# A transformer layer with routed experts on one core: two raw weight loads ordered behind accumulating transfers

## What is computed

```python
q = (h @ peer_wq).reshape(B, T, PEER_HEADS, PEER_QDIM)        # 8 heads x 256
q1, q2 = q[..., :PEER_HALF], q[..., PEER_HALF:]
s1 = jnp.einsum('bthd,nd->bthn', q1, sub_keys1, ...)          # 128 keys each
s2 = jnp.einsum('bthd,nd->bthn', q2, sub_keys2, ...)
v1, i1 = lax.top_k(s1, PEER_TOPK)
v2, i2 = lax.top_k(s2, PEER_TOPK)
cand_s = v1[..., :, None] + v2[..., None, :]                  # 16 x 16 candidates
top_s, pos = lax.top_k(cand_s, PEER_TOPK)
eid = jnp.take_along_axis(cand_i, pos, axis=-1)
gate = jax.nn.softmax(top_s, axis=-1)
...
a = gelu(einsum('td,tkd->tk', hb, peer_u[eb]))
out = einsum('tk,tkd->td', gb * a, peer_v[eb])
```

## Time and profile before

| what | value |
|---|---|
| runs shown | 984.2, 985.12, 985.66 us; median 985.12 |
| profiled execution, own time | 982.17 us |
| its span, first to last instruction | 980.4 us |
| busy: TensorE, VectorE, ScalarE, GpSimd | 960.9, 751.0, 465.6, 193.8 us |
| chain that ended last, largest shares | TensorE 75%; lines L1851 36%, L1831 20%, L1834 10%, L1790 6% |
| granted clock of TensorE | 0.997 |

### The profile page before, as it was taken

The page is one execution under the profiler, slowest core; times in us unless marked ns, Lnnn a source line. Parts: engine busy times, 40 slices in busy tenths (PEclk is TensorE's granted clock), DMA queues, the critical chain, the costliest instruction groups (busy, mean ns, idle before and its releaser), DMA issues.

```text
span 980.4 us, 16912 instructions
## 1 busy us (share of the span) xinstructions
PE 960.9 (98%) x5616; PEld 844.3 (86%) x5616; DVE 751.0 (77%) x1385; ACT 465.6 (47%) x718; POOL 193.8 (20%) x234
## 2 busy tenths in 40 slices
PE   7999999899999999999999999999999999999998
PEld 7998899898999888888888888888888888888886
DVE  5799767998988887777767777777767777777766
ACT  5566545433777534434444444434444444434442
POOL 4074227986887100000000000000000000000000
PEclk9999999999999999999999999999999999999999
DMA  8543129845222776555555545555555555555554
GB/s 264 171 129 122 52 88 332 199 99 166 80 56 59 244 239 226 173 199 187 185 200 176 209 173 204 179 195 190 181 204 176 208 173 201 184 189 196 176 209 150
DMA packets 70164, 172.57 MB, mean 176 GB/s; under 512 B 6752, under 2 KB 35552, under 8 KB 69616
## 3 DMA queue, kind: packets, MB, share of 16 engines
q1 hardware_dynamic: 68080, 167.47, 50.6%
q0 software_dynamic: 576, 4.19, 2.1%
q10 hardware_dynamic: 1472, 0.44, 0.2%
HBM read 163.16 MB, written 4.72 MB: 171 GB/s over the span
## 4 chain that ended last, share of the span: by engine, by line
PE 75%; DVE 1%; issue 0%; DVEq 0%; POOL 0%
PE psum L1851 36%; PE psum L1831 20%; PE psum L1834 10%; PE psum L1790 6%; PE psum L1797 2%; PE psum L1721 1%; DVE big L1129 0%; PE psum L1480 0%; DVE big L1273 0%; DVE big L1140 0%; PE psum L1778 0%; DVEq L102 0%; DVE big L1175 0%; POOL big L1376 0%; DVE big L1171 0%
## 5 line engine op out<-in xcount | busy, mean ns | idle before, releaser
L1851 PE MATMUL psum<-rr 128*128 128x512 f32 x1536 | 369.1, 391 | 0.0
L1851 PEld LDWEIGHTS psum<-rr 128*128 128x128 f32 x1536 | 288.0, 188 | 59.1
L1831 PE MATMUL psum<-h_all,rr 128*128 128x512 f32 x856 | 306.6, 392 | 0.0
L1195 DVE TENSOR_TENSOR rr<-raw,rr 128x1024 fp32r<-128x1024 f32 x109 | 133.6, 1226 | 144.9 <-ACT rr L757 144.9
L757 ACT ACTIVATE rr<-raw 128x1024 fp32r<-128x1024 f32 x109 | 115.5, 1060 | 270.2 <-PE psum L1851 270.2
L1834 PE MATMUL psum<-h_all,rr 128*128 128x256 f32 x856 | 221.9, 280 | 0.0
L1831 PEld LDWEIGHTS psum<-h_all,rr 128*128 128x128 f32 x856 | 160.6, 188 | 32.2 <-DVE rr L1134 0.6
L1834 PEld LDWEIGHTS psum<-h_all,rr 128*128 128x128 f32 x856 | 160.8, 188 | 8.2
L645 ACT ACTIVATE rr<-raw 128x1024 fp32r<-128x1024 f32 x107 | 113.6, 1062 | 66.2 <-DMA raw<-in_peer_u_dram 62.1
L1134 DVE TENSOR_TENSOR rr<-raw,rr 128x1024 fp32r<-128x1024 f32 x107 | 130.6, 1221 | 3.9 <-ACT rr L645 1.8
L1181 DVE TENSOR_TENSOR rr<-psum,picks 128x2048 fp32r<-128x2048 f32 x32 | 72.4, 2288 | 9.3 <-PE psum L1790 7.6
(11 more groups left out here) (205 smaller groups left out, 952.5 us busy)
## 6 DMA issues: line engine op xcount, KB each, us to landing
raw<-in_peer_u_dram SPq DMA_DIRECT2D x128, 512.0 KB, 4.1
raw<-in_peer_v_dram SPq DMA_DIRECT2D x128, 512.0 KB, 3.6
big<-in_w_in_dram SPq DMA_DIRECT2D x10, 1024.0 KB, 6.1
big<-in_peer_wq_dram SPq DMA_DIRECT2D x8, 1024.0 KB, 6.2
big<-in_w_out_dram SPq DMA_DIRECT2D x4, 1024.0 KB, 5.2
rr<-big POOLq DMA_DIRECT2D x4, 1024.0 KB, 8.2
up_kept<-gel SPq DMA_DIRECT2D x20, 128.0 KB, 3.6
gel<-up_kept SPq DMA_DIRECT2D x20, 128.0 KB, 3.8
```

Of the source, the lines that this page charges most:

```text
L1195: dve.tensor_tensor(v_sp[s][:, 1, :], v_raw[s], f(v_sp[s][:, 0, :]), ALU.subtract).then_inc(v_lo, 1)
L1831: return pe.matmul(both, ut[s][:, 0, k, :], ht[:, :, k, :], start=(k == 0), stop=(k == DK - 1))
L1851: i = pe.matmul(psum[:, 4 + 2 * t + n, :], g_sp[:, s, x, t * P:(t + 1) * P], v_sp[s][:, y, n * 512:(n + 1) * 512], start=(first and m == 0 ...
```

## The change

SyncE no longer issues the raw load of head 6 ahead of the loop. Inside the loop, after `keep_early(0)`, it waits for the landing of the first addition and then issues the load of head 6; after `keep_early(1)` it waits for the landing of the second addition and then issues the load of head 7. On GpSimd the second addition moves from behind the multiplies of head 1 to ahead of them, and the third from behind both multiplies of head 2 to between them. The fourth stays. What is computed is the same.

```diff
             load_w(WQ0 + 5)
-            load_w(WQ0 + 6)
             for e in range(EARLY):
                 keep_early(e)
-                if e == 1:
-                    load_w(WQ0 + 7)
+                if e < 2:
+                    sp.wait_ge(ld_neg[e], 16)
+                    load_w(WQ0 + 6 + e)
...
                 pool.wait_ge(p_cide, g + 1)
-                if g == 0:
-                    add_low(0)
+                if g < 2:
+                    add_low(g)
                 pool.wait_ge(d_match, g + 1)
                 tiles = 2 if g < PH - 1 else 1
                 for t in range(tiles):
+                    if g == 2 and t == 1:
+                        add_low(2)
                     i = pool.tensor_tensor(eqs[:, s, t], ...)
...
                 if g == 0:
                     candidates(1)
-                elif g < len(ADDED_Q):
-                    add_low(g)
+                elif g == 3:
+                    add_low(3)
```

## The result

The change made the kernel slower: 988.42 us median (20 runs) against 985.12 (20 runs), ratio 1.0035 with a 95% interval from 1.0025 to 1.0046. That is 3.3 us the wrong way, where 0.3 us the right way was forecast.

A forecast was written before the change was run, and what follows sets the result against it. TensorE's matmul chain bounds the kernel, with VectorE setting the pick stage's end. Of 1.8 us gained at head 5, 0.1 stayed at head 6; VectorE ended 0.3 sooner: 985.12 - 0.3 = 984.8 us, range 982.9 to 987.7.

The forecast's parts named there:

- What bounds the kernel: TensorE's matmuls behind the picks; VectorE sets the pick stage's end, and TensorE waits 3.97 us for additions ahead of heads.
- First addition: Ahead of head 4: without head 6's load in front it lands sooner, giving back 0.51 us; head 4 starts at 174.40.
- rival D: First addition waits for something other than the load, its landing stays at 174.8; 0.2 to 0.7 us lost; chance 0.10.
- Load of head 6: Behind the first landing: issued about 173.8, landed 180.3, before ScalarE wants it at 180.84; costs nothing.
- Second addition: Ahead of head 5: issued at 176.28, lands at 186.0 (bounds 184.65 to 186.5), 1.8 us sooner.
- wrong altogether: Sign: second addition lands after 187.8 or head 6's load reaches ScalarE after 181.5; stage 1 to 3 us later.
- Load of head 7 and third addition: Load issued 186.1, lands 192.6, costs about nothing; addition issued 186.8, lands 197.6, a new 1.7 us wait at head 6.
- My rule: An addition queued behind a raw load lands 5.0 us after that load; applied to the second and third additions.
- behind the ring load as well: Third addition, ahead of head 6, queued behind head 7's load and the ring load too: lands at 198.8.
- rival C: Third addition holds up head 7's load by 5.1 us, head 7 starts 3.2 us later; 3.2 us lost; chance 0.23.
- Rival B: Additions do not queue behind what SyncE sent; 2.1 us gained, 983.0 us; chance 0.22.
- ceiling: With every transfer running clean, GpSimd's schedule limits head 7; no more than 2.3 us gained, 982.8 us.

The follow-up runs named there:

- e1_sync_part: The kernel before with only SyncE's part of the change, GpSimd's additions left as they were; 1.0034 of the time before.
- e8_third_later: The changed kernel with the third addition back behind both multiplies of head 2; 1.0040 of the time before.
- e12_rings_last: e4_head6_sooner with SyncE's next ring loads and stores held until the fourth addition landed, and that addition issued between two multiplies; 979.50 us against 984.24 before.
- e4_head6_sooner: The changed kernel with the load of head 6 issued ahead of the loop again, as before; 0.9985 of the time before.
- e10_changed_again: The changed kernel unaltered, run again on another run's chip and profiled a second time; 986.83 us, 1.0037 of the time before.

## Why the prediction was wrong

*What bounds the kernel* held: a delay before the transposes of the picks is one at the end, and ScalarE's and GpSimd's waits pass through TensorE's scores to VectorE.

*First addition.* Wrong in size. It was to land in 7.6 to 8.0 us with head 6's load gone; it took 8.7, and 8.7 to 9.3 in all the runs, whether that load stood ahead of it or not. The wait ahead of head 4 was 0.33 us after the change and 0.30 to 0.88 in the other runs, so the 0.51 us were not to be had. The load was not its cause, as rival D had it; what is, was not tried (in every run a ring load went out 1.5 us ahead of it).

*Load of head 6* landed in 6.3 us, ScalarE never waited for it: right.

*Second addition.* The step that failed first. I took 186.0, with an upper bound of 186.5; on the axis of the changed execution these are 185.0 and 185.5, and it landed at 186.88. That is the prediction's own sign of being wrong altogether (after 187.8, on this axis 186.8). Nearly each term was short. The load ahead of it went out at 173.59, 0.8 us later than reckoned, because the first addition was late, and landed 6.3 us later, at 179.9. The ring load landed at 174.01 + 7.6 = 181.6, 1.7 us behind the load and not 1.2; the addition came 5.3 us after that, not 5.0. The mechanism was right (the addition ran behind what was ahead of it, the ring load too), and the 1.8 us that were to be gained on head 5 were nothing.

*Load of head 7 and third addition.* The step that decided. I had the load 0.7 us ahead and TensorE waiting 1.7 us for the addition. Since the second addition landed 1.9 us later than reckoned, and the load went out 1.8 later with it and the third addition only 0.5, the load followed the third addition by 0.56 us, and the load paid. My rule, taken from one row with a lead of 2.97 us, was used for a pair 0.7 us apart, and what it gave was itself too small: with a lead of 0.9 to 1.05 us an addition lands 12.3 to 12.7 us after issue, not the 10.8 that I took (197.6 - 186.8). My case "behind the ring load as well" (198.8, 12.0 us after issue) was the nearer one. With this pair in either order the runs lost 3.3 to 3.9 us by the estimates, 1.9 or more by the intervals (`e1_sync_part`, `e8_third_later` and the change itself: 1.0034, 1.0040, 1.0035); none shows the forecast's 0.3 us gained, and 0.23 for rival C was too low. (The sixth early block, whose ring load waits behind this load, starts at 212.97 in the trace of before, not after 215; nobody waited for it all the same.)

*Rival C's price* was right for the load (5.1 us; 5.2 measured), and its chain is the one that came. The rest of its sum was not: the load itself went out 1.8 us later than C had it, so on the axis of before the fourth addition went out at 204.4 and not at 202.6, and TensorE began head 7 at 211.6 and not at 210.4, 4.4 us later than before instead of 3.2 (4.5 in the second profile). That C's 3.2 us in all agrees with the 3.3 between the medians is in part luck, since the profile of before that the lengths are taken from is 2.95 us below its median. *Rival B* did not come about: no addition passed a load or a ring load that had been issued 1.7 us or more ahead of it. The *ceiling* of 2.3 us was a ceiling for this edit with GpSimd's schedule as it was; `e12_rings_last` goes past it (4.7 us between the medians, 3.8 by the ratio with 2.3 to 5.3 as its interval) with the fourth addition moved up and the ring loads held. The two profiled executions differ by 2.9 us (982.17 and 979.23), 2.6 of them in this stage; where the rest of the medians' 4.7 comes from was not settled.

*The clock* was not in the prediction. It belongs in a profile's reading, but the runs with idle matmuls do not show the change's loss coming from it.

## What to carry to other kernels

Putting a transfer behind the landing of another ties its start to that landing, late or not: look at what else goes out within a microsecond or two of it, since two 1 MB transfers that meet cost one of them, or both, about 5 us here. Look at the packets as well: taking turns one for one, the transfer with packets of 1 KB stood nearly still beside the one with 8 KB. Count everything already on its way ahead of a transfer in full, 512 KB ring loads included, and move the transfers that nobody waits for behind the last one that somebody does. A profile of one execution can show a cost (here 2.5 us of half clock) that another execution has elsewhere or not at all: time a run that takes it away before putting it on the bill.

## What the runs showed of the hardware that was not expected

An addition of 1 MB with nothing beside it lands in 6.9 to 7.1 us (`e12_rings_last`), not the 7.6 that before showed at best; the raw load with nothing beside it in 5.5.

TensorE's granted clock fell to the lower level after several pauses in this stage, but not after all of like length. The products of a head, 5.9 us otherwise, took 7.4 to 8.6 after pauses of 2.11 (`e4_head6_sooner`), 2.62 (`e10_changed_again`), 2.90, 3.07, 3.11, 3.35, 3.44 and 5.04 us, and 5.9 after pauses of 2.64 (before), 2.69 (`e8_third_later`), 3.05 (changed kernel) and 3.54 (`e10_changed_again`). The granted clock reads 0.50 to 0.71 in a stretch of 3 to 6 us of the slow ones and 1.00 in those of the others. With idle matmuls in the pause they took 5.8 to 5.9 each time.
